# Forming the scan's skip term on VectorE instead of GpSimd, in a two-block transformer kernel on one Trainium2 core

## What is computed

```
X = x * dt                                   # per head
CB = C @ B.T                                 # per group and chunk, 128 x 128
y_diag = (CB * Lmat) @ X                     # Lmat: decay of each head, exp of cumulated steps
y_off = (C @ state) * exp(a_cum)             # second chunk only: state of the first chunk
y = y_diag + y_off
y = y + d_skip[head] * x                     # the skip term
y = y * silu(z)
y = rmsnorm(y per group) * norm_g
out = y @ w_branch
```

## Time and profile before

| | |
|---|---|
| Median of three runs | 1191.82 us (1191.3 to 1192.6) |
| Profiled execution | 1191.22 us, its span 1189.4 us |
| Mean granted TensorE clock | 0.98 of full |
| PE busy | 1135.6 us, 95% |
| DVE busy | 693.6 us, 58% |
| ACT busy | 587.9 us, 49% |
| POOL busy | 23.5 us, 2% |
| The skip term on POOL (L856) | 8 instructions, 8.7 us |

### The profile page before, as it was taken

The page is one execution under the profiler, slowest core; times in us unless marked ns, Lnnn a source line. Parts: engine busy times, 40 slices in busy tenths (PEclk is TensorE's granted clock), DMA queues, the critical chain, the costliest instruction groups (busy, mean ns, idle before and its releaser), DMA issues. The chain is left out here.

```text
span 1189.4 us, 13875 instructions
## 1 busy us (share of the span) xinstructions
PE 1135.6 (95%) x5748; PEld 952.0 (80%) x5748; DVE 693.6 (58%) x777; ACT 587.9 (49%) x830; POOL 23.5 (2%) x35
## 2 busy tenths in 40 slices
PE   5999999999999999999899999999998889999997
PEld 4888887999989877777778888878887777888886
DVE  4644545676677777766575544466755266644443
ACT  4543335454577656654363444266565444444333
POOL 0000000000001100000000000000000000000000
PEclk9999999899999999999999999999998699999999
DMA  9666564555666553355456655545632235656650
GB/s 312 200 194 191 182 191 145 192 178 179 185 199 191 181 187 115 119 166 195 142 177 194 195 178 185 198 137 179 189 131 71 71 116 181 198 178 184 202 180 36
DMA packets 131150, 202.74 MB, mean 170 GB/s; under 512 B 5728, under 2 KB 98784, under 8 KB 130832
## 3 DMA queue, kind: packets, MB, share of 16 engines
q1 hardware_dynamic: 128272, 190.68, 49.9%
q0 software_dynamic: 2816, 11.18, 2.7%
HBM read 200.76 MB, written 1.08 MB: 170 GB/s over the span
## 5 line engine op out<-in xcount | busy, mean ns | idle before, releaser
L898 DVE TENSOR_TENSOR WL<-RAW,WH 128x2048 fp32r<-128x2048 f32 (+1 forms) x181 | 406.0, 2265 | 101.0 <-ACT WH L432 100.8
L432 ACT ACTIVATE WH<-RAW 128x2048 fp32r<-128x2048 f32 (+1 forms) x181 | 338.5, 1890 | 15.1 <-DMA RAW<-in_w_in 6.8
L1440 PE MATMUL PS<-WH,XTH 128*128 128x512 f32 (+1 forms) x700 | 277.7, 397 | 1.9 <-ACT V L622 1.9
L1442 PE MATMUL PS<-WH,XTL 128*128 128x512 f32 (+1 forms) x700 | 273.4, 391 | 0.0
L1441 PE MATMUL PS<-WL,XTH 128*128 128x512 f32 (+1 forms) x700 | 272.7, 390 | 0.0
L1440 PE MATMUL ACC<-WH,KTH 128*128 128x512 f32 (+1 forms) x466 | 186.9, 401 | 9.2 <-DVE KTL L987 6.0
L1441 PE MATMUL ACC<-WL,KTH 128*128 128x512 f32 (+1 forms) x466 | 184.0, 395 | 0.0
L1442 PE MATMUL ACC<-WH,KTL 128*128 128x512 f32 (+1 forms) x466 | 184.0, 395 | 0.0
L1440 PEld LDWEIGHTS PS<-WH,XTH 128*128 128x128 f32 x700 | 131.7, 188 | 28.2 <-ACT V L622 2.3
L1442 PEld LDWEIGHTS PS<-WH,XTL 128*128 128x128 f32 x700 | 131.5, 188 | 27.9
L1441 PEld LDWEIGHTS PS<-WL,XTH 128*128 128x128 f32 x700 | 131.8, 188 | 25.7
(11 more groups left out here) (258 smaller groups left out, 1287.3 us busy)
## 6 DMA issues: line engine op xcount, KB each, us to landing
RAW<-in_w_in SPq DMA_DIRECT2D x48, 1024.0 KB, 5.3
RAW<-in_ffn_w_gate SPq DMA_DIRECT2D x44, 512.0 KB, 4.0
RAW<-in_ffn_w_up SPq DMA_DIRECT2D x44, 512.0 KB, 5.0
RAW<-in_ffn_w_down SPq DMA_DIRECT2D x22, 1024.0 KB, 5.0
RAW<-in_w_gate SPq DMA_DIRECT2D x22, 512.0 KB, 4.1
RAW<-in_w_up SPq DMA_DIRECT2D x22, 512.0 KB, 5.1
RAW<-in_w_down SPq DMA_DIRECT2D x11, 1024.0 KB, 5.0
RAW<-in_ssd_w_branch SPq DMA_DIRECT2D x8, 1024.0 KB, 5.1
```

Of the source, the lines that this page charges most:

```text
L432: nc.scalar.activation(WH[:, s, 0:n], RAW[:, s, 0:n], ACT.Copy).then_inc(w_hi, 1)
L898: tt(WL[:, s, 0:n], RAW[:, s, 0:n], WH[:, s, 0:n].bitcast(F32), ALU.subtract).then_inc(w_lo, 1)
L1440: mm(ps, stat_hi, mov_hi, start=first, stop=False)
L1442: return mm(ps, stat_lo, mov_hi, start=False, stop=last)
```

## The change

The skip term leaves POOL's program and is formed by DVE, between x times dt (and its decayed form) and the sum with the matmuls. POOL keeps the eight DMAs. `skip_ok` is no longer used; DVE's new wait is for `ys_ok`, which DVE itself raised one step earlier.

```diff
@@ -844,18 +844,7 @@
             for r in range(8):
-                g, c = divmod(r, 2)
-                if r == 0:
-                    spread_cum(0)
-                if r < 7:
-                    spread_cum(r + 1)
-
-                if r:
-                    pool.wait_ge(ys_ok, r)
-                skip = ROWS[:, ROW["skip"] + g * HPG:ROW["skip"] + (g + 1) * HPG]
-                nc.gpsimd.tensor_tensor(Y.rearrange("p (h c) -> p h c", h=HPG),
-                                        BUF1[:, c, g * GW:(g + 1) * GW].rearrange("p (h c) -> p h c", h=HPG),
-                                        skip.unsqueeze(2).to_broadcast([P, HPG, SSD_P]), ALU.mult).then_inc(skip_ok, 1)
+                spread_cum(r)
 
@@ -1115,7 +1104,10 @@
                 if r:
                     n = r - 1
                     g, c = divmod(n, 2)
-                    dve.wait_ge(skip_ok, r)
+                    skip = ROWS[:, ROW["skip"] + g * HPG:ROW["skip"] + (g + 1) * HPG]
+                    if n:
+                        dve.wait_ge(ys_ok, n)
+                    own.link(tt(by_head(Y), by_head(BUF1[:, c, g * GW:(g + 1) * GW]), heads_bc(skip), ALU.mult))
                     dve.wait_ge(ssd_y, r)
                     own.link(tt(Y, PS[3][:], Y, ALU.add))
```

## The result

The changed kernel takes 1196.97 us, median of six runs (1194.05 to 1198.0); the kernel before took 1190.09 us, median of six (1188.13 to 1192.6). The ratio is 1.0054 with a 95% interval of 1.0036 to 1.0072: slower. In a second session the same kernel came out at 1.0034 (1.0022 to 1.0046). The profiled execution took 1196.26 us with a span of 1194.4 us, 5.0 more than the 1189.4 of before.

What follows compares the result with a forecast made beforehand. The DVE-ACT chain, with 0.41 us slack in 22.98, reaches PE through its wait for V's copy. Lag 3.35 plus clock 1.7 made 5.1 us, on 1191.82 giving 1196.9 us, range 1193.6 to 1199.0.

Steps and rivals of the forecast that it cites:

- POOL's eight terms removed: Skip terms taken off POOL in the scan: DVE never waited for skip_ok, so worth 0.
- the port: POOL's SBUF reads slowing DVE: steady terms fall in DVE's idle time, so 0; rival of hidden contention 3%.
- The first skip term's contention: Ahead of step 1, POOL's term slowed DVE's split by 0.45 us once; removing it gives nothing, PE holds step 1.
- Eight terms on DVE: Each added term behind L1111 costs DVE 0.725 us, bounds 0.28 and 1.03; rival of a cheap term 6%.
- Six terms less two holes: Steps 1 to 6, ahead of V's copy: 4.35 us less 0.50 us DVE idle at steps 3 and 5, 3.35 us.
- The late starts: DVE's lag at the starts of steps 3, 5 and 6: 0.94, 1.90 and 2.63 us.
- The wait: PE's one wait in the scan, for ACT's copy of V, grows from 1.92 to 5.3 us, ending near 419.9.
- The margin at step 5: DVE's decay product would end at 404.23, just before PE wants it at 404.42, so no new PE wait.
- Steps 7 and 8: Terms behind PE's wait make DVE and ACT 1.45 us later; idle time behind absorbs it, costed at 0.
- the cover: Idle time behind step 8, ACT's 1.69 us and DVE's 1.42 us, absorbing 1.45 us; without it 1.45 us is paid.
- The clock: Behind PE's 5.3 us wait: 1.2 GHz for 3.4 us, losing 1.7 us, bounds 0 and 3.4; rival of none 12%.
- the rivals' own sums: Unseen slack without slow clock, 1193.3 us (a third of 15%); longer low clock or further stalls, 1198.5 us (20%).

Runs made afterwards that it cites:

- e3: Kernel before with the skip term left out on both engines, the sum on DVE adding silu(z) in its place; ratio 1.0000.
- e2: Kernel before, POOL's terms kept, plus a second skip term on DVE at the change's place, written to an unread scratch tile; ratio 1.0044.
- e8: Changed kernel with 20 unread 128x512 matmuls on PE ahead of the wait for the copy of V; ratio to before 1.0032.
- e9: Kernel before with DVE forming the skip term at steps 1 and 2 only, POOL the other six; ratio 1.0004.
- e10: Kernel before with DVE forming the skip term at steps 5 and 6 only, POOL the others; ratio 1.0034.
- e11: Kernel before with DVE forming the skip term at steps 7 and 8 only, POOL the others; ratio 1.0005.
- e6: Changed kernel with the second V projection's second tile in PSUM bank 0, not 5, so PE needs no copy of V; ratio 1.0021.
- e7: Changed kernel with DVE's skip term moved behind the gated norm, ahead of the split, and V's tile in PSUM bank 0; 1188.66 us, ratio 0.9983.
- e4: Changed kernel run again as it is; ratio to the kernel before 1.0034.
- e1: Changed kernel with DVE's skip term moved behind the gated norm, ahead of the split, issued with own.inc instead of own.link; ratio 1.0008.

## Why the prediction was right

*POOL's eight terms removed, 0; the port, 0.* Shown by e3 and e2. The first skip term's contention of 0.45 us gave nothing back, as foretold: in the changed kernel that split takes 2.29 us, and DVE then idles 2.08 us for ACT before its next product with the decay, where it idled 1.62.

*Eight terms on DVE at 0.725.* The trace has 0.69 us each, and the way from L1100 to L1112 grew by 0.71 to 0.72 at steps 3, 5 and 6; the nearest row (L1111) was the right one to take.

*Six terms less two holes, 3.35 us.* The profile after has 3.31, e8 has 3.35, and e9 and e10 each show their part. The late starts at steps 3, 5 and 6 were put at 0.94, 1.90 and 2.63, and are 0.93, 1.88 and 2.59. The wait was to end near 419.9; less the 0.74 us of the start it ends at 419.81.

*The margin at step 5.* L1126 of step 5 ends at 404.94 and PE's L1657 starts at 405.16 with no wait. It held with 0.2 us to spare.

*Steps 7 and 8, 0.* Shown by e11, and the changed kernel itself used nearly all of the cover, as the forecast had it: ACT's idle time there fell from 1.69 to 0.23 us.

```profile
448.29 0.60 ACT L611 ACTIVATE BUF<-PS 128x512 f32<-128x512 f32 x1 [0.23 <-PE PS L1434]
```

In e6, where PE arrives earlier, the cover failed, and 2.04 and 0.82 us of waits stand behind the scan.

*The clock, 1.7 us: a term mis-sized.* The mechanism was right (e8), the size was 2.75 to 2.79 in the scan: the low clock lasted 6.8 us and not 3.4. That was the upper bound of the term, 3.4 us, less what fell into the wait. With it the sum would be 3.35 + 2.8 = 6.1, and the measured differences are 1190.09 x 0.0054 = 6.4 us and, in the second session, 1191.43 x 0.0034 = 4.1 us. The forecast of 5.1 lies between. That the time itself comes out within 0.1 us, 1196.9 against 1196.97, is luck: the kernel before was put at 1191.82 by three runs and is 1190.09 by six, 1.73 lower, while the difference of the medians is 6.88 and not 5.1. The two errors cancel. (The range's ends, 1193.6 and 1199.0, are also 0.3 and 0.5 above the rivals' own sums, 1193.3 and 1198.5; the measured time lies well inside either way.)

*What the prediction did not see: the rest of the span is not constant.* I wrote that all stages behind the scan would be as long as before. They are 745.46 us in the profile after and 749.15 in the second profile of the same kernel. In the first, the stall of 3.00 us at 581.82 has no low clock behind it (the line of 582 to 587 above reads 1.00); in the second the same stall, 3.00 us at 581.83, has:

```profile
582.00:587.00 5.00, 5.00 (x18) 0.66 0.21 73
```

A low stretch of 3.4 us loses 1.7 us of full speed. Behind this stall of 3.00 us it is there in 9 of the 13 profiles and missing in 4 (after, e6, e7, e9), and the profiles do not show why. So the 5.0 us between the two spans are 0.74 of start, 6.10 of the scan, and 1.84 given back by chance. The spread of the runs goes with the clock as well. In the session with 35 runs of the kernel before (1188.2 to 1193.9 us), the 11 runs with a mean granted clock of 0.985 have a mean of 1188.7 us, the 16 with 0.980 or 0.981 have 1191.9, and the 7 with 0.979 or less 1192.5. What sets it off in one run and not in another stays open.

## What to carry to other kernels

An engine at 58% may have 0.4 us to spare in 23: look for the chain that goes to and fro between two engines, and count only the idle time in it that waits for the bottleneck. Put added work in the idle time that waits for the partner (here ahead of the split, where it cost 0.1 us at most), not between the bottleneck's signal and what is handed on. And where an added lag meets an engine whose clock falls when it idles, price the clock with it: here 3.3 us of wait cost 6.1. And when one stage is measured by two marks in the trace, set the second mark behind the low clock: e6 seemed to cost 1.6 us by the one and cost 4.6 by the other.

## What the runs showed of the hardware

- At the wait for V, TensorE's low clock lasted 3.4 us behind waits of 2.4 and 3.4 us (e9, e10) and 6.8 us behind 5.2 and 5.3 us (after, e2, e4); there was none behind 1.9 and 2.0 us (before, e1, e3, e11). Behind the same stall of 3.00 us it came in 9 of 13 profiles.
- Matmuls without use, put in a wait, kept the clock at 2.4 GHz and made the scan 2.75 us shorter (e8). Taking the wait away by another bank gave 2.2 us in the kernel before, for a wait of 1.92. In the changed kernel the filling was worth more than the bank: to the stall, 3.35 us above before (e8) against 4.59 (e6).
